# Norms without pair sums and filling products, one norm for two in the middle, and the next block's split ahead of the residual

## The reference

```
first block:   x += 0.5*swiglu(rms(x)*g);  x += mlstm/sgu mixer(rms(x)*g);  x += 0.5*swiglu(...);  x = rms(x)*g_final
second block, twice: x += 0.5*g1*swiglu(h1); x += g2*mixer(h2); x += 0.5*g3*swiglu(h3)
               h = rms(x)*norm_g*(1+scale) + shift,   scale, shift, g1..g3 from silu(c) @ mod_w + mod_b
last:          rms(x)*final_norm_g
rms(x) = x * rsqrt(mean(x*x) + 1e-6)  per token
```

## Time and profile before

| | |
|---|---|
| median of 3 runs | 1699.43 us (1697.11 to 1700.32) |
| profiled execution | 1698.5 us, span 1696.7 us |
| PE busy | 1662.9 us, 98% |
| PE weight loads busy | 1627.7 us, 96% |
| DVE / ACT busy | 1202.4 us, 71% / 809.9 us, 48% |
| mean granted PE clock | 0.996 |

### The profile page before, as it was taken

How to read it: one execution, slowest core, us unless ns; L and a number is a source line. 1 busy time by engine, 2 the same in 40 slices (tenths; PEclk the granted TensorE clock), 3 DMA queues, 4 the chain that set the end, 5 groups by cost and what they waited for, 6 DMA issues and landing times.

```text
span 1696.7 us, 34452 instructions
## 1 busy us (share of the span) xinstructions
PE 1662.9 (98%) x14542; PEld 1627.7 (96%) x14542; DVE 1202.4 (71%) x1303; ACT 809.9 (48%) x874; POOL 87.1 (5%) x110
## 2 busy tenths in 40 slices
PE   9999999999999999999998899999999999999998
PEld 9999999999999999999997899999999987899998
DVE  5888876676788887888867688756545566765444
ACT  5444456654544444444565553445444456554442
POOL 0000000000000000000004000000000003200000
PEclk9999999999999999999999999999999999999999
DMA  7988744344498875988533359653654443335551
GB/s 311 346 331 312 279 174 174 125 166 158 146 354 318 303 276 187 340 312 320 205 141 125 125 201 345 247 188 135 224 197 175 174 148 125 125 141 208 198 189 59
DMA packets 50491, 365.08 MB, mean 215 GB/s; under 512 B 5728, under 2 KB 5856, under 8 KB 6240
## 3 DMA queue, kind: packets, MB, share of 16 engines
q1 hardware_dynamic: 39744, 287.04, 46.0%
q0 software_dynamic: 10368, 75.50, 12.0%
q10 hardware_dynamic: 288, 1.18, 0.2%
HBM read 362.65 MB, written 1.05 MB: 214 GB/s over the span
## 4 chain that ended last, share of the span: by engine, by line
PE 88%; DVE 7%; ACT 3%; issue 1%; DMA 0%; SPq 0%; ACTq 0%; DVEq 0%
PE bank L252 50%; PE bank L284 24%; PE bank L267 3%; PE bank L244 3%; DVE wlo L184 2%; PE bank L357 2%; PE bank L1662 1%; PE bank L369 1%; DVE m_p L1427 0%; DVE m_e L1924 0%; ACT whi L176 0%; DVE x L309 0%; ACT m_e L1803 0%; DVE x L401 0%; PE bank L1231 0%
## 5 line engine op out<-in xcount | busy, mean ns | idle before, releaser
L184 DVE TENSOR_TENSOR wlo<-raw,whi 128x2048 fp32r<-128x2048 f32 x261 | 598.1, 2294 | 203.0 <-ACT whi L176 202.2
L252 PE MATMUL bank<-xh,whi 128*128 128x256 f32 x2608 | 728.0, 279 | 3.4 <-ACT gate L533 2.0
L252 PE MATMUL bank<-xl,whi 128*128 128x256 f32 x2608 | 723.3, 277 | 0.0
L252 PE MATMUL bank<-xh,wlo 128*128 128x256 f32 x2608 | 723.0, 277 | 0.0
L176 ACT ACTIVATE whi<-raw 128x2048 fp32r<-128x2048 f32 x261 | 498.4, 1913 | 312.5 <-PE bank L252 190.9
L252 PEld LDWEIGHTS bank<-xh,whi 128*128 128x128 f32 x2608 | 492.1, 189 | 6.1 <-issue 2.6
L252 PEld LDWEIGHTS bank<-xl,whi 128*128 128x128 f32 x2608 | 490.7, 188 | 0.1
L252 PEld LDWEIGHTS bank<-xh,wlo 128*128 128x128 f32 x2608 | 490.7, 188 | 0.0
L284 PE MATMUL bank<-hid_hi,whi 128*128 128x256 f32 x1056 | 292.8, 277 | 0.0
L284 PE MATMUL bank<-hid_lo,whi 128*128 128x256 f32 x1056 | 291.9, 276 | 0.0
L284 PE MATMUL bank<-hid_hi,wlo 128*128 128x256 f32 x1056 | 291.9, 276 | 0.0
(11 more groups left out here) (317 smaller groups left out, 1822.7 us busy)
## 6 DMA issues: line engine op xcount, KB each, us to landing
raw<-stream_in SPq DMA_DIRECT2D x270, 1024.0 KB, 4.8
mod_raw<-mod_in POOLq DMA_DIRECT2D x72, 1024.0 KB, 7.0
params<-params_in SPq DMA_DIRECT2D x1, 1474.0 KB, 16.1
x<-x_in SPq DMA_DIRECT2D x2, 512.0 KB, 4.3
m_gsu<-sgu_in ACTq DMA_DIRECT2D x1, 1024.0 KB, 5.1
y_out<-x SPq DMA_DIRECT2D x1, 1024.0 KB, 3.8
consts<-consts_in SPq DMA_DIRECT2D x1, 280.5 KB, 4.8
tab_pos<-pos_in ACTq DMA_DIRECT2D x1, 128.0 KB, 3.5
```

Source lines behind the costliest of these rows:

```text
L184: dve.tensor_tensor(wlo[:, s, :], raw[:, s, :], whi[:, s, :].bitcast(F32), ALU.subtract)\
L252: last = pe.matmul(out[:, m, :], (whi, wlo)[wp][:, s, k * 256 + m * P:k * 256 + m * P + P], (xh, xl)[ap][:, k, :], start=(k == 0 and j == ...
```

## The change

- The column sums take each squared tile by itself: 16 small products per norm, not 8, and no DVE pair sum. Norm 0 keeps its pairs.
- The bf16 products in the norms are gone. The last bf16 product of each ffn turn stays, and so do 60 at the program's start.
- Norm 3 is no phase of its own on PE and ACT: norm 4 computes both roots, from the sums of x*x and of (g_final*x)^2; the scaled x that the first block hands on is written by DVE late in phase 4 (`dve_final_inside`).
- The split of the next phase's second block is a whole one, made on ACT and DVE in the last output block, before the residual.
- In mix2 and mix3 the shift is no longer added to `xm`: ACT and DVE add it on the way to `xh` and `xl`, and two more columns of `xm` carry it through the small products, whose result gets it as a bias.
- SP waits for x before it issues the second and third weight block; the gains `gmod` and `gres` are computed behind the `xl` products' operands.

```
-            act_split_halves(act, n + 1)          # end of act_ffn, mix phases alike
+            act_split(act, F0 + 34)
...
+            if n == AFTER_FINAL:
+                dve_final_inside(dve)
             if groups < 5:
                 turns(groups, 5, False)
             dve_split(dve, F0 + 33)
+            dve_split(dve, F0 + 34)
             if groups:
                 mod_store()
...
-        WARM = (14, 8, 14, 26)
...
         def pe_norm(pe, n):
...
             for b in range(4):
-                if b >= 2:
-                    pe_keep_warm(pe, n, WARM[b - 2])
-                pe.wait_ge(sem("x_paired"), 4 * n + b + 1)
-                for tt in range(2):
-                    mm = pe.matmul(STAT[:, T + tt:T + tt + 1], xm[:, 2 * b, tt * P:tt * P + P], ones[:, 0:1],
...
+                if n == 0:
+                    pe.wait_ge(sem("x_paired"), b + 1)
+                    mm = column_sums(xm, 2 * b, T, b == 0, b == 3)
+                    continue
+                pe.wait_ge(sem("x_squared"), 4 * ni + b + 1)
+                for k in (2 * b, 2 * b + 1):
+                    mm = column_sums(xm, k, T, k == 0, k == KD - 1)
+                if n == AFTER_FINAL:
+                    for k in (2 * b, 2 * b + 1):
+                        pe.wait_ge(sem("final_step"), k + 1)
+                        mm = column_sums(final_squares, k, T + 2, False, k == KD - 1)
             mm.then_inc(sem("x_summed"), 1)
-            pe_keep_warm(pe, n, WARM[2])
...
-            if phases[n][0] != "final":
-                pe_keep_warm(pe, n, WARM[3])
...
         def dve_norm(...):
+            if n == AFTER_FINAL:
+                dve.tensor_scalar(std[:, 0:2], STAT[:, T:T + 2], RMS_EPS, float(D), ALU.add, ALU.mult)
+                dve.scalar_tensor_tensor(out=std[:, 2:4], in0=std[:, 0:2], scalar=RMS_EPS, in1=STAT[:, T + 2:T + 4],
+                                         op0=ALU.mult, op1=ALU.add)
...
-            def add_shift(k):
-                dve.tensor_scalar(xm[:, k, :], xm[:, k, :], shift[:, k:k + 1], None, ALU.add)
...
+            if phases[n][0] in ("mix2", "mix3"):
+                dve.tensor_copy(xm_wide[:, :, T:W], shift.unsqueeze(2).to_broadcast([P, KD, 2]))
...
         def mod_fold():
+                if n == AFTER_FINAL:
+                    pe.wait_ge(sem("x_updated"), 4 * n)
...
         def dt():
-                    mm = pe.matmul(MODP[0:16, 0:T], prm("w_dt")[:, k * 16:k * 16 + 16], xm[:, k, :],
+                    mm = pe.matmul(MODP[0:16, 0:W], prm("w_dt")[:, k * 16:k * 16 + 16], xm_wide[:, k, :],
...
-            for n in range(min(SLOTS, N_BLOCKS)):
+            sp.dma_start(raw[:, 0, :], a_stream[0:P, :]).then_inc(sem("w_loaded0"), 16)
+            sp.wait_ge(sem("x_loaded1"), 16)
+            for n in range(1, SLOTS):
```

More of the change, by code:

```diff
@@ L31 @@
 T = 256
+W = T + 2
 D = 1024
@@ L187, in build_program, with act_split_halves, dve_split_halves @@
         H = BLK // 2
[L191 to L227, removed]
+        def act_split_halves(act):
+            act.wait_ge(sem("w_loaded0"), 16)
+            act.activation(whi[:, 0, 0:H], raw[:, 0, 0:H], ACT.Copy).then_inc(sem("w_half_ready"), 1)
+            act.activation(whi[:, 0, H:BLK], raw[:, 0, H:BLK], ACT.Copy).then_inc(sem("w_hi_ready"), 1)
+        def dve_split_halves(dve):
+            dve.wait_ge(sem("w_half_ready"), 1)
+            dve.tensor_tensor(wlo[:, 0, 0:H], raw[:, 0, 0:H], whi[:, 0, 0:H].bitcast(F32), ALU.subtract)
+            dve.wait_ge(sem("w_hi_ready"), 1)
+            dve.tensor_tensor(wlo[:, 0, H:BLK], raw[:, 0, H:BLK], whi[:, 0, H:BLK].bitcast(F32), ALU.subtract)\
+               .then_inc(sem("w_lo_ready"), 1)
         PASSES = ((0, 0), (0, 1), (1, 0))
@@ L377, in pe_norm @@
             mm.then_inc(sem("rstd_spread"), 1)
-            if phases[n][0] != "final":
-                pe_keep_warm(pe, n, WARM[3])
-            elif n + 1 < len(phases):
-                pe_keep_warm(pe, n, 60)
-        def dve_norm(dve, n, g, shift=None, split=True, whole=False):
-            if n == 0:
-                for b in range(4):
-                    dve_pair(dve, n, b)
-            dve_split_half(dve, n, 0)
-            dve.wait_ge(sem("std_ready"), n + 1)
-            dve.reciprocal(rstd[:, 0:2], std[:, 0:2]).then_inc(sem("rstd_ready"), 1)
-            dve_split_half(dve, n, 1)
-            dve.wait_ge(sem("rstd_spread"), n + 1)
+            if n == AFTER_FINAL:
+                for tt in range(2):
+                    mm = pe.matmul(MODP[:, tt * P:tt * P + P], rstd[:, tt:tt + 1].to_broadcast([P, P]), ident,
+                                   start=(tt == 0), stop=True, skip_group_check=True)
+                mm.then_inc(sem("final_step"), 1)
@@ L462, in dve_phase_norm @@
                 layer, j = MOD_OF[n]
-                dve.wait_ge(sem("gmod_ready"), 1 + sum(m < n for m in MOD_OF))
-                dve_norm(dve, n, gmod, mod_col(layer, j), whole=phases[n][0] != "ffn")
+                dve.wait_ge(sem("gmod_ready"), 2 + sum(m < n for m in MOD_OF))
+                dve_norm(dve, n, gmod, mod_col(layer, j))
             else:
-                dve_norm(dve, n, prm(GAIN_OF[n]), None, split=(n not in (3, 10)))
+                dve_norm(dve, n, prm(GAIN_OF[n]), None, split=(n != 10))
         def dve_phase_residual(dve, n):
@@ L1113, in dve_mix1 @@
             merged_rest(3)
-            for b in range(3):
+            for b in range(4):
                 dve_split(dve, F0 + MIX1_IN + 2 + b)
@@ L1511, in dve_mix2 @@
             rest(3)
-            for b in range(3, MIX2_OUT - 1):
+            for b in range(3, MIX2_OUT):
                 dve_split(dve, F0 + MIX2_IN + 2 + b)
@@ L2046, in _ @@
             dve.memset(cols[:, 65:66], LN_EPS).then_inc(sem("eps_ready"), 1)
+            for b in range(4):
+                dve_pair(dve, b)
             dve.wait_ge(sem("consts_loaded"), 32)
```

177 lines of the change are left out of this document (103 added, 74 removed).

## The result

| | before | changed |
|---|---|---|
| median | 1698.33 us (1697.11 to 1700.32, 4 runs) | 1721.60 us (1719.19 to 1723.24, 4 runs) |
| ratio, 95% interval | | 1.0131 [1.0113, 1.0148] |
| profiled execution, its span | 1698.5, 1696.7 | 1722.6, 1720.9 |
| PE busy | 1662.9 | 1669.5 |
| DVE busy | 1202.4 | 1183.0 |

The changed kernel is 23 us slower, 1.3%, and the interval does not reach 1. DVE has 19 us less to do, as the change means it to, and PE is busy 7 us longer although all the bf16 products in the norms are gone.

A forecast was written before the change was run, and what follows sets the result against it. It took TensorE, 88% of the chain, to bound the kernel. Its terms, -3.0 us with the clock untouched and +27.1 for clock falls, gave +24.1 on 1698.5: 1722.6, stated as 1723 us, range 1695 to 1732.

The forecast's parts named there:

- the likeliest case: Whole kernel: the granted clock falls in each norm without bf16 products; 1723 us, 1712 to 1732, chance 0.72.
- Sums: Each norm's column sums without pair sums: 32 loads, 3.64 us where 3.04 pass now, +0.6 per norm.
- Opening: Start of the kernel: sums end at 11.8, reciprocal 12.7, first product 15.2 against 18.52; -3.3, then +2.1 for a cold block.
- Clock: Falls about 3.1 us after the last dense product; 4.4 us cold dense work, half lost; 3.0 per norm, +27.1 in all.
- The joined norm: The two middle norms as one: 64 loads in 7.1 us, -4.1; the clock's fall adds +6.7.
- Norm 2: Early split +0.85; clock -0.6, since most hides in the 2.0 us gate wait, whose own fall may go (-1.6).
- Norm 5: Late scaling of x on DVE delays the residual to 827.4: +3.1-0.3-1.7=+1.1, plus 3.0 for the clock.
- Norm 8: Residual begins 2.7 later behind the whole split, +0.85; shift additions gone, -1.7; clock's fall, 3.0.
- The shift: In the mixers DVE no longer adds the shift: -1.7 at norms 5 and 8; its column costs +0.3.
- The whole split: Next block's split on DVE before the residual delays the squares: +0.85 at norms 2, 6, 8, 9, +0.35 at 1 and 7.
- the column sums hold the clock: Rival: one-column sums count as work, only the opening's +2.1 comes on top: 1697.6 us, 1695 to 1702, chance 0.16.
- faster: Rival: the clock holds and DVE's early split is hidden, sum -5.1: 1693.4 us, chance 0.12.

The follow-up runs named there:

- e2: The kernel before with each group of bf16 products replaced by fp32 matmuls of one moving column, keeping TensorE busy about as long: 1736.5 us, ratio 1.0222.
- e9: The changed kernel with bf16 products back in the opening, behind the sums and behind the spread; column sums stay one column wide: 1721.4 us, ratio 1.0114.
- e4: The changed kernel with column sums 64 moving columns wide and the bf16 products back in the idle stretches: 1701.2 us, ratio 1.0011.
- e5: The kernel before with the block after next split whole ahead of the residual, no longer in halves inside the norm: 1715.7 us, ratio 1.0084.
- e6: The kernel before without pair sums behind the opening, so all eight squares get one-column sums; products behind sums and spread stay: 1712.8 us, ratio 1.0091.
- e7: The changed kernel with 64-column sums, bf16 products back, and DVE's whole split moved behind the residual, ahead of the reciprocal: 1694.6 us, ratio 0.9979.
- e1: The kernel before without the bf16 products that pass the time in its norms, nothing else changed: 1708.5 us, ratio 1.0066.
- e3: The changed kernel with column sums 64 moving columns wide instead of one, no bf16 products put back: 1707.4 us, ratio 1.0052.

## Why the prediction was right, and which terms of it were not

The forecast was 1723 us for the likeliest case, measured 1721.6; its own sum was +24.1 on the profiled execution and 24.2 came. The mechanism is shown: the clock falls in every norm of the changed kernel; e2 and e9 show that neither one-column filling nor bf16 products around one-column sums hold it, and e4, which differs from e9 in the columns alone, holds it in all norms but the opening and norm 5. The agreement of the total is partly luck, since terms were off on both sides. I had -3.0 for the change with the clock untouched and +27.1 for the clock. By the medians e4 is 1.3 us above the kernel before and 20.4 below the changed kernel. e4 is not quite the change with the clock untouched (in its profile norm 5 still loses it), so these are estimates of the two terms, but they put the clock some 7 us lower and the rest some 4 us higher than I did, and the two misses nearly cancel. By column of the table, forecast first: opening -1.2 / -1.6; norm 1 +3.4 / +3.2; norm 2 +0.3 / +2.5; joined +2.6 / -1.4; norm 5 +4.1 / +6.3; norm 6 +3.9 / +2.4; norm 7 +3.4 / +2.6; norm 8 +2.2 / +4.7; norm 9 +3.9 / +4.5; norm 10 +1.5 / +1.0; and +0.3 for the shift column, which I had not placed.

*Sums.* 3.64 us forecast, 3.65 measured in norms 1, 6, 7, 9 and 10: right. In norms 2, 5 and 8 the clock fell inside them, and they took 4.9 to 6.6. I had let every fall come some 3.1 us behind the last dense product; in the changed kernel it came 2.4 us (norm 8) to 5.1 us (norm 9) behind it. In norms 1, 6, 7, 9 and 10 that was behind the sums, so that my 0.3 for their end was not lost there, and in 2, 5 and 8 more was.

*Opening.* First product at 15.2 forecast, 15.30 measured; the reciprocal at 12.78, where I had 12.7. Those were right, the way there was not. I took the clock to be at half from the start, and the sums to end at 11.8. Windows of the changed kernel's weight loads, and the sums:

```profile
6.00:9.40 3.40, 2.02 (x25) 1.00 1.05 424
9.40:15.30 5.90, 2.12 (x11) 0.50 1.04 435
```

```profile
8.19 2.41 PEld L338 LDWEIGHTS bank<-consts,xm 128*128 128x128 f32 x16 [1.38 <-issue]
```

The clock had risen by 6.00, and the sums end at 10.60; that changes nothing, because the reciprocal waits for DVE's halves. My evidence on what holds the clock was this opening in one execution of the kernel before. e5 and e6 have the same opening, and in their profiles the clock was full from 5.2 and 5.7 to 8.6 and 9.2 and back at 18.8 and 16.0: the reading was weaker than I took it for, and it is e4 and e9 that bear it out.

*Clock.* It fell in every norm and stayed down for 6.8, 10.2 or 13.7 us; the mean is 0.970, where I had "near 0.98". 4.4 us of cold dense work was my figure: it was 3.8 to 4.6 in the opening and in norms 2 and 5 to 9, 5.5 in norm 1 and 1.1 in the joined one. Read at the end of the first block, norms 1, 6, 7 and 9 cost 3.2, 3.4, 2.9 and 3.7 us against 3.4, 3.9, 3.4 and 3.9 forecast; the rest of norm 6's miss, 1.1, lies in the unchanged work behind it.

*The joined norm* is a term of the wrong size. The clock held for 4.2 us of the sums (633.21 to 637.45), where I let it fall after 3.1, so some 25 loads ran cold and not 36: the sums took 9.9 us, not 11.1. And as most of the low stretch lay in sums and waits, dense work at the half clock was 1.1 us, and 0.6 was lost for my 2.2. That makes 2.8 of the miss of 4.0; about 1.0 of the rest lies in the phase behind it and is not explained.

*Norm 2.* The forecast was 3.9 us at the end of the first block, of which the gate wait gives back 3.6, its 2.0 idle and the 1.6 of its own clock fall. Measured are 4.9, because the clock fell at 442.89 inside the sums and held them to 445.61, and only 2.3 came back. ScalarE around the gate, before:

```profile
455.08 0.42 ACT L1582 ACTIVATE cos<-tab_angle 128x256 f32<-128x256 f32 x1 [1.69 <-DVE tab_angle L1577]
455.51 1.28 ACT L533 ACT_TABLE_LOAD   x1
456.81 0.60 ACT L533 ACTIVATE gate<-bank 128x512 f32<-128x512 f32 x1
```

and in the changed kernel:

```profile
458.65 0.42 ACT L1580 ACTIVATE cos<-tab_angle 128x256 f32<-128x256 f32 x1 [1.69 <-DVE tab_angle L1575]
459.09 1.28 ACT L526 ACT_TABLE_LOAD   x1
460.38 0.60 ACT L526 ACTIVATE gate<-bank 128x512 f32<-128x512 f32 x1
```

The first block of the phase ends 6.4 us later on the span's clock (456.22 against 449.80), the gate only 3.6: it follows ScalarE's cosine, which waits for DVE's `tab_angle`, and a table load, not PE. So PE isn't idle there any more and the granted clock is 1.00 in all windows from 457 to 466. The direction was right; both sizes were off, and in the same sense.

*Norm 5.* "The residual begins at 827.4, 3.1 later" was right against PE (3.4 later), but I priced it as a delay of the sums alone. PE stood idle 2.6 us for it (828.96 to 831.59), the clock fell at 832.01, 0.4 us into the sums, and these took 6.55 us. e7 parts the two causes: with the split behind the residual and the late scaling of x still in place, the residual begins 1.2 us ahead of the last output product (2.45 in the kernel before), so the scaling makes 1.2 of the 3.4 and the split 2.2. The scaling's part costs 0.5 in e7 (12.4 us from the last output product to the first block's end, 11.9 to 12.0 in e7's other norms). The split's place alone parts e4 from e7, and with it norm 5 goes from +6.1 to -0.2 in their profiles. Its rows on DVE in the changed kernel (answers to the earlier trace rows):

```profile
825.31 4.48 DVE L187 TENSOR_TENSOR wlo<-raw,whi 128x2048 fp32r<-128x2048 f32 x2
...
829.94 3.23 DVE L286 SCALAR_TENSOR_TENSOR x<-bank,gres,x 128x256 f32<-128x256 f32 x8
```

*Norm 8.* Residual "2.7 later": 1.14 us ahead of the last output product and not 3.78, 2.6 later. Right. The rest of the miss has two sources: the clock fell inside the sums (5.24 us), and further on in the same phase it fell once more at the end of an idle piece of 2.30 us ahead of 1405.72, which was 2.08 before and had left the clock alone. That is 1.6 us, and not the change's doing: kernels without the change have it too in some executions (e2 and e5 in their profiles).

*The shift.* -1.7 in norms 5 and 8 for leaving DVE's additions out can be read only where the clock holds: scaling to the xl products is 4.96 us in norm 5 of e7 (824.75 to 829.71) against 6.49: -1.5.

*The whole split* I priced at +0.85 in norms 2, 6, 8 and 9. The profile of e5, its slowest run, has it with the pair sums in place: 1.0 and 1.9 in norms 1 and 7, where the clock holds, and 2.7 to 5.6 in those four norms, where the clock falls at the norm (the 5.6 of norm 8 has in it one more fall further on, as above). By its four runs the waits cost some 11 us and the clock's answer 5 to 13 more. This is the step that was wrong in kind: a wait of PE was counted at its length, while the clock's answer to it can cost as much again. It did little harm to the total, because each norm had a fall in its price already.

*The rival "the column sums hold the clock"* is refuted by e2 and e9. By the Trainium skill, TensorE: Matmul & The Clock Gate (Why this matters for your kernels), throughput drops when PE idles between bursts of matmuls. In the joined norm here the clock fell without an idle piece, and in e2 it fell behind 2.5 us in which PE's loads were busy for 2.42 and stayed down through 6.80 us of a busy PE, so the measurement decides against reading it by the letter. *The rival "faster"* needed the early split to be hidden; e5 refutes that.

## What to carry to other kernels

Where PE does many weight loads for one moving column each (sums over partitions), widen the moving operand as long as the load sets the pace: here 64 columns cost nothing and were worth 20 us of 1721 together with the products, while the products alone were worth nothing that could be measured beside one-column sums (they were worth 8.6 us in the kernel before). Price a wait of PE with the clock's answer to it and not by its length, and look for the place where DVE or ScalarE waits anyway (here ahead of the reciprocal) before moving work ahead of what PE waits for. And look at the joined sums: two reductions of the same data with different weights are one matmul with two moving columns.

## What the runs showed of the hardware that I had not expected

- A 128x128 f32 weight load takes 0.111 us with one moving column and with 64 (32 loads in 3.65 us in both), and 0.22 us at the half clock (eight in 1.83 or 1.78): loads scale with the granted clock. The Trainium skill, TensorE: Matmul & The Clock Gate (LDWEIGHTS (loading the stationary operand)), gives a load's time in ns as its columns over 1.2, so 107 for 128; the 0.111 us agrees with it at the full level, the 0.22 us at the half one does not.
- Filling an engine can be dearer than leaving it idle: e2 against e1, +28 us.
- The granted clock fell to half in the middle of 9.9 us of gapless sums (637.45), and in e3 with 64 columns it fell in no sums behind the opening but those of norm 5, ahead of which PE had waited 2.6 us.
